# The modulation matrix summed in three column passes instead of four, and c laid out to the partitions by transfers instead of matrix products

## What is computed

```
silu_c = jax.nn.silu(c)                                    # c * sigmoid(c), 2048 values
sh1, sc1, g1, sh2, sc2, g2 = jnp.split(silu_c @ w_mod + b_mod, 6)      # w_mod: 2048 x 12288
h = modulate(rms_norm(x, norm_g[0]), sh1, sc1)
x = x + g1 * rms_norm(fourier_mix(h) @ fnet_w_out, norm_g[1])
x = x + g2 * rms_norm(sqrelu_mlp(modulate(rms_norm(x, norm_g[2]), sh2, sc2), w_mlp_in, w_mlp_out), norm_g[3])
```

## Time and profile before

| | |
|---|---|
| runs, median (lowest to highest) | 1681.84 us (1681.52 to 1683.0) |
| profiled execution, span from first to last instruction | 1678.7 us; of this execution the page gives the span alone |
| PE, DVE, ACT busy | 1667.0 us, 1190.8 us, 858.7 us |
| TensorE clock granted | 9 (full) in each of the 40 slices of the span |
| read from HBM | 404.58 MB, 242 GB/s over the span |

### The profile page before, as it was taken

The page is one execution under the profiler, slowest core; times in us unless marked ns, Lnnn a source line. Parts: engine busy times, 40 slices in busy tenths (PEclk is TensorE's granted clock), DMA queues, the critical chain, the costliest instruction groups (busy, mean ns, idle before and its releaser), DMA issues.

```text
span 1678.7 us, 22570 instructions
## 1 busy us (share of the span) xinstructions
PE 1667.0 (99%) x9084; PEld 1444.9 (86%) x9084; DVE 1190.8 (71%) x1291; ACT 858.7 (51%) x1212; POOL 21.3 (1%) x34
## 2 busy tenths in 40 slices
PE   9999999999999999999999999999999999999997
PEld 9899888888989988888898888888888888888886
DVE  7878777887868777798678577777655455546555
ACT  7667556444656655644464564434443444334442
POOL 0000000000100000000000000000000000000000
PEclk9999999999999999999999999999999999999999
DMA  9689676997777777799639478887655665566553
GB/s 333 215 274 313 218 272 226 335 356 279 247 258 253 267 238 263 240 346 370 228 125 334 151 226 282 294 286 245 196 176 200 187 190 197 210 196 188 189 200 126
DMA packets 218120, 408.16 MB, mean 243 GB/s; under 512 B 9088, under 2 KB 87200, under 8 KB 217248
## 3 DMA queue, kind: packets, MB, share of 16 engines
q1 hardware_dynamic: 217520, 404.58, 70.3%
q10 hardware_dynamic: 496, 2.14, 0.3%
HBM read 404.58 MB, written 2.11 MB: 242 GB/s over the span
## 4 chain that ended last, share of the span: by engine, by line
PE 97%; issue 1%; DVE 1%; ACT 0%; DMA 0%; POOL 0%; DVEq 0%; POOLq 0%; SPq 0%; ACTq 0%
PE banks L455 96%; PE banks L1663 1%; PE banks L1625 0%; DMA modw<-in_w_mod 0%; PE banks L1634 0%; DVE X L1104 0%; DVE X L1532 0%; PE banks L1821 0%; POOL sc L674 0%; ACT junk L712 0%; DVE modacc L1139 0%; ACT junk L723 0%; ACT swap L809 0%; ACT vtmp L1017 0%; ACT vtmp L1007 0%
## 5 line engine op out<-in xcount | busy, mean ns | idle before, releaser
L451 DVE TENSOR_TENSOR wlo<-raw,whi 128x1024 fp32r<-128x1024 f32 (+2 forms) x561 | 663.4, 1189 | 375.0 <-ACT whi L444 372.1
L444 ACT ACTIVATE whi<-raw 128x1024 fp32r<-128x1024 f32 (+2 forms) x561 | 573.4, 1030 | 578.4 <-PE banks L455 542.6
L455 PE MATMUL banks<-H,whi 128*128 128x512 f32 x2048 | 660.0, 398 | 0.7 <-DVE H L1062 0.7
L455 PEld LDWEIGHTS banks<-H,wlo 128*128 128x128 f32 x2048 | 384.9, 188 | 88.5
L455 PE MATMUL banks<-whi,Y 128*128 128x512 f32 x1472 | 455.6, 389 | 0.0
L455 PE MATMUL banks<-H,wlo 128*128 128x256 f32 x2048 | 402.6, 278 | 0.0
L455 PEld LDWEIGHTS banks<-whi,Y 128*128 128x128 f32 x1472 | 276.3, 188 | 57.7 <-DVE wlo L451 0.2
L455 PEld LDWEIGHTS banks<-H,whi 128*128 128x128 f32 x2048 | 317.0, 189 | 1.9 <-issue 0.8
L455 PE MATMUL banks<-wlo,Y 128*128 128x512 f32 x768 | 298.8, 389 | 0.0
L1139 DVE SCALAR_TENSOR_TENSOR modacc<-modw,cvx,modacc 128x1024 f32<-128x1024 f32 x188 | 240.4, 1279 | 9.7 <-DMA modw<-in_w_mod 9.4
L455 PEld LDWEIGHTS banks<-wlo,Y 128*128 128x128 f32 x768 | 144.2, 188 | 29.8
(11 more groups left out here) (224 smaller groups left out, 1343.5 us busy)
## 6 DMA issues: line engine op xcount, KB each, us to landing
modw<-in_w_mod SPq DMA_DIRECT2D x192, 512.0 KB, 6.5
raw<-in_w_in SPq DMA_DIRECT2D x72, 1024.0 KB, 5.4
raw<-in_w_mlp_in SPq DMA_DIRECT2D x64, 1024.0 KB, 5.5
raw<-in_w_mlp_out SPq DMA_DIRECT2D x64, 1024.0 KB, 5.0
raw<-in_w_o SPq DMA_DIRECT2D x32, 1024.0 KB, 7.1
raw<-in_w_fnet SPq DMA_DIRECT2D x16, 1024.0 KB, 5.1
raw<-in_w_mv SPq DMA_DIRECT2D x7, 1024.0 KB, 6.3
raw<-in_w_mk SPq DMA_DIRECT2D x6, 1024.0 KB, 6.1
```

The source lines that it names most:

```text
L444: nc.scalar.activation(hi_part(step, n), raw[u % RAW][:, (step % 2) * n:(step % 2) * n + n], ACT.Copy).then_inc(hi_ready, 1)
L451: nc.vector.tensor_tensor(wlo[u % RAW][:, part], raw[u % RAW][:, part], hi_part(step, n).bitcast(F32), ALU.subtract).then_inc(lo_ready, 1)
L455: return nc.tensor.matmul(o, a, b, start=start, stop=stop, skip_group_check=True)
```

## The change

- `MOD_PASS` has three passes: eight pieces of 1024 columns side by side for columns 0 to 8191 (128 units of 16 rows), then two passes of two pieces as before. The sums stand at steps 255 (step 111 of layer 1), 310 and 421.
- c is loaded ten times by SP, each time with the 128 partitions in the order that the units need: eight transfers for the eight-piece layout and two for the two-piece one. In each the source repeats a row for the partitions that share it. ACT and DVE make silu from all 160 columns, straight into `cvx`.
- The six products on PE, the copy on ACT and the two `alike` copies on DVE go. `sel` has 8 + 2 columns.

```diff
-MOD_PASS = ((0, 4, 0), (2 * D, 2, 64), (3 * D, 4, 96), (5 * D, 2, 160))
+MOD_PASS = ((0, 8, 0), (4 * D, 2, 128), (5 * D, 2, 160))
...
-                                sp.dma_start(cv[:, 0:KT], cvec).then_inc(c_in, 16)
+                                for c0, groups in ((0, 8), (8, 2)):
+                                    for j in range(groups):
+                                        rows_of = cvec[j * P // groups:(j + 1) * P // groups, :]
+                                        sp.dma_start(c_rows[:, (c0 + j) * KT:(c0 + j + 1) * KT],
+                                                     rows_of.unsqueeze(1).broadcast_to([P // groups, groups, KT])).then_inc(c_in, 16)
...
-                        act.wait_ge(c_in, 16)
-                        nc.scalar.activation(cv[:, KT:2 * KT], cv[:, 0:KT], ACT.Exp, scale=-1.0).then_inc(c_exp, 1)
-                    if l == 0 and s == CV_AT[3]:
-                        act.wait_ge(cv_T, 1)
-                        nc.scalar.activation(cvx[:, :], M[2][:, 0:96], ACT.Copy).then_inc(cv_ready, 1)
+                        act.wait_ge(c_in, 160)
+                        nc.scalar.activation(c_gate[:, :], c_rows[:, :], ACT.Exp, scale=-1.0).then_inc(c_exp, 1)
...
-                co = (0 if groups == 4 else 64) + j - j0
+                co = (0 if groups == 8 else 8 * KT) + (j - j0) % groups * KT + (j - j0) // groups
...
-                        for e0, groups in ((0, 4), (4, 2)):
-                            nc.vector.tensor_reduce(sel[:, e0:e0 + groups], ident[:, :].rearrange("p (i e) -> p e i", e=groups), AX_X, ALU.add)
-                            w = nc.vector.tensor_copy(alike[:, P * e0:P * (e0 + groups)].rearrange("p (i e) -> p i e", e=groups),
-                                                      ident[:, :].unsqueeze(2).broadcast_to([P, P, groups]))
+                        for e0, groups in ((0, 8), (8, 2)):
+                            w = nc.vector.tensor_reduce(sel[:, e0:e0 + groups], ident[:, :].rearrange("p (i e) -> p e i", e=groups), AX_X, ALU.add)
...
-                    if l == 0 and s == CV_AT[2]:
-
-                        pe.wait_ge(cv_step, 3)
-                        pe.wait_ge(sel_set, 1)
-                        for c0, e0, groups in ((0, 0, 4), (64, 4, 2)):
-                            for j in range(groups):
-                                i = mm(M[2][:, c0 + j:c0 + groups * KT:groups], alike[:, (e0 + j) * P:(e0 + j + 1) * P],
-                                       cv[:, 2 * KT:], True, True)
-                        i.then_inc(cv_T, 1)
```

More of the change, by code:

```diff
@@ L211 @@
 MOD_END = {c: step for step, c in MOD_SUM.items()}
-CV_AT = (4, 5, 9, 10)
+CV_AT = (4, 5)
 ANG_AT = (6, 8, 12, 15)
 GATE_ROW = (114, 116, 118, 121)
-assert MOD_END[1] < LH + GATE_ROW[0] and MOD_END[2] < BY_TOKEN[1]
+assert MOD_END[0] < LH + GATE_ROW[0] and MOD_END[1] < BY_TOKEN[1]
 IDLE = 24
@@ L324, in build_program @@
         ones = at("ones", [P, 8], m + 0.5)
-        sel = at("sel", [P, 8], m + 0.53125)
         gs = at("gs", [P, G_CONST], m + 0.5625)
-        alike = at("alike", [P, 6 * P], A + 50)
+        c_rows = at("c_rows", [P, 10 * KT], A + 50)
+        c_gate = at("c_gate", [P, 10 * KT], A + 51)
         modT = at("modT", [P, NMOD * KT], m + 0.8125)
@@ L335, in build_program @@
         A2 = at("A2", [P, KT], m + 1.6875)
-        cv = at("cv", [P, 3 * KT], m + 1.75)
-        ropev = at("ropev", [P, 2], m + 1.9375)
-        sc = at("sc", [P, 96], m + 1.96875)
+        sel = at("sel", [P, 10], m + 1.75)
+        ropev = at("ropev", [P, 2], m + 1.8125)
+        sc = at("sc", [P, 96], m + 1.84375)
         SS, MS, RS = 0, 4, 8
@@ L345, in build_program @@
         PS, PN, XP, XN = 64, 5, 80, 3
-        cvx = at("cvx", [P, 96], m + 2.34375)
-        assert origin + (m + 2.71875) * 1024 <= nc.sbuf_top
+        cvx = at("cvx", [P, 10 * KT], m + 2.21875)
+        assert origin + (m + 2.84375) * 1024 <= nc.sbuf_top
         banks = ctx.enter_context(nc.psum_tensor("banks", [P, 8, 512], F32))
@@ L355, in build_program @@
         pair = [flat_banks[:, 1024 * i:1024 * (i + 1)] for i in range(4)]
-        MODCOL = 480
+        MODCOL = 448
         def bank(g):
@@ L395, in build_program @@
         x_copied, x_sum, conv_in, conv_out = map(sem, ("x_copied", "x_sum", "conv_in", "conv_out"))
-        sel_set, cv_T, cv_ready = sem("sel_set"), sem("cv_T"), sem("cv_ready")
+        sel_set = sem("sel_set")
         x2_T0, x2_T1, x2_hi0, x2_lo0 = map(sem, ("x2_T0", "x2_T1", "x2_hi0", "x2_lo0"))
@@ L1128, in mod_unit @@
                 dve.wait_ge(mod_in[j % MRING], 16 * (j // MRING + 1))
-                co = (0 if groups == 4 else 64) + j - j0
+                co = (0 if groups == 8 else 8 * KT) + (j - j0) % groups * KT + (j - j0) // groups
                 co = cvx[:, co:co + 1]
                 if j == 0:
-                    dve.wait_ge(cv_ready, 1)
+                    dve.wait_ge(cv_step, 3)
                 if j == j0:
@@ L1284, in _ @@
                         dve.wait_ge(c_exp, 1)
-                        nc.vector.tensor_scalar(cv[:, KT:2 * KT], cv[:, KT:2 * KT], 1.0, None, ALU.add).then_inc(cv_step, 1)
+                        nc.vector.tensor_scalar(c_gate[:, :], c_gate[:, :], 1.0, None, ALU.add).then_inc(cv_step, 1)
                         dve.wait_ge(cv_step, 1)
-                        nc.vector.reciprocal(cv[:, 2 * KT:], cv[:, KT:2 * KT]).then_inc(cv_step, 1)
+                        nc.vector.reciprocal(cvx[:, :], c_gate[:, :]).then_inc(cv_step, 1)
                         dve.wait_ge(cv_step, 2)
-                        tt(cv[:, 2 * KT:], cv[:, 2 * KT:], cv[:, 0:KT], ALU.mult).then_inc(cv_step, 1)
+                        tt(cvx[:, :], cvx[:, :], c_rows[:, :], ALU.mult).then_inc(cv_step, 1)
                         dve.wait_ge(ident_in, 16)
-                        for e0, groups in ((0, 4), (4, 2)):
-                            nc.vector.tensor_reduce(sel[:, e0:e0 + groups], ident[:, :].rearrange("p (i e) -> p e i", e=groups), AX_X, ALU.add)
-                            w = nc.vector.tensor_copy(alike[:, P * e0:P * (e0 + groups)].rearrange("p (i e) -> p i e", e=groups),
-                                                      ident[:, :].unsqueeze(2).broadcast_to([P, P, groups]))
+                        for e0, groups in ((0, 8), (8, 2)):
+                            w = nc.vector.tensor_reduce(sel[:, e0:e0 + groups], ident[:, :].rearrange("p (i e) -> p e i", e=groups), AX_X, ALU.add)
                         w.then_inc(sel_set, 1)
@@ L1392, in _ @@
                     if l == DEPTH - 1 and s == GATE_ROW[0]:
-                        dve.wait_ge(mod_out, 2)
+                        dve.wait_ge(mod_out, 1)
                         tt(R[:, 0:KT], mod(2), ng(1), ALU.mult).then_inc(r_ready, 1)
@@ L1440, in _ @@
                     scaled_rows(acc[i % 2], rowb, i, 2 * (4 * DEPTH + i)).then_inc(acc_dve, 1)
-            dve.wait_ge(mod_out, 3)
+            dve.wait_ge(mod_out, 2)
             nc.vector.scalar_tensor_tensor(A2[:, :], mod(4), 1.0, ng(2), ALU.add, ALU.mult)
@@ L1489, in _ @@
                     if q == 2 and s == 2:
-                        dve.wait_ge(mod_out, 4)
+                        dve.wait_ge(mod_out, 3)
                         tt(R[:, KT:], mod(5), ng(3), ALU.mult).then_inc(r_ready, 1)
@@ L1586, in mod_sums @@
                 pe.wait_ge(sel_set, 1)
-                own = sel[:, 0:4] if groups == 4 else sel[:, 4:6]
+                own = sel[:, 0:8] if groups == 8 else sel[:, 8:10]
                 for t in range(8):
@@ L1618, in _ @@
                             pe.wait_ge(x_xn, 2 * l + 2)
-                            pe.wait_ge(cv_ready, 1)
                             sums_read(base + s)
@@ L1825, in _ @@
             by_token(1, acc[1], (Hhi, Hlo))
-            pe.wait_ge(mod_out, 3)
+            pe.wait_ge(mod_out, 2)
             pe.wait_ge(acc_dve, DVE0 + 3)
```

## The result

The changed kernel takes **1751.76 us** (median of five runs, 1748.23 to 1761.24), the kernel before 1681.8 (1681.5 to 1683.0). The ratio is 1.0425, interval 1.0409 to 1.044: slower by 70 us where 1.9 us less was forecast. The profiled execution is the longest of the five, 1761.24 with a span of 1759.4 us.

What follows compares the result with a forecast made beforehand. The prediction took TensorE (PE), busy 99% of the span, to bound the kernel. Products -1.34, sum pass -1.80 and delay +1.2 summed to -1.9 us, giving 1679.9 us, range 1678.2 to 1682.8.

Steps and rivals of the forecast that it cites:

- At nothing: Items priced at zero: copies removed on ACT and DVE, three longer DVE operations, the reshaped w_mod loads, moved steps.
- the four rivals: Alternative outcomes: 1678.7 us (chance 0.20), 1681.3 (0.10), 1696.6 (0.06) and 1681.7 (0.09).
- The chance of slower, 0.08: Probability given to a time over 1685.20 us, slower by more than 0.2%.
- SP's issue: Rival at c's ten transfers: slow issues on SP's queue delay step 8's unit by 17.9 us, 1696.6 us; chance 0.06.
- a fixed cost of the small transfers: Rival: each of nine extra transfers costs the DMA engines 0.29 us, delay 2.6, kernel 1681.3 us; chance 0.10.
- The sum pass, -1.80: PE in attention, step 63 of layer 1: one of four passes of eight sum products goes, -1.80 us.
- rival 4: In attention, step 63 of layer 1, softmax sets the pace and the sum's 1.80 us return: 1681.7 us; chance 0.09.
- The products, -1.34: PE at about 31.5 us: the six products that lay c out go, -1.34 us.
- The delay d, +1.2: Step 8 of layer 0: c's ten transfers make the w_mk unit land later, PE stands still, +1.2 us (ends 0 and 1.8).
- the page's figure, 1684.8: Kernel time in us if nine more small transfers cost 6.1 us, estimated by the skill page; not the forecast.
- a gap above 3 us at step 8: Sign of being wrong: PE's gap at step 8, 0.15 us before and forecast about 1.3, exceeds 3 us.
- new waits of PE after step 14: Sign of being wrong: PE shows waits after step 14 that the kernel before did not have.

Runs made afterwards that it cites:

- the control of the last: Kernel before with one unit of w_mod moved from step 50 to step 63 in layer 0 alone: 1681.05 us, ratio 0.9993.
- the fourth: Kernel before without the products, four passes, c's transfers behind unit 7's load, one w_mod unit moved from step 50 to 63 in both layers: 1683.47 us.
- its control: Kernel before with one unit of w_mod moved from step 50 to step 63 in both layers, nothing else: 1684.14 us, ratio 1.0013.
- the first experiment: Changed kernel with the four passes of before, c still laid out by transfers, six in place of ten: 1681.31 us, ratio 0.9998.
- the changed kernel with fast loads: Changed kernel with first-pass loads of 32 half rows of four pieces, from other columns of w_mod, in place of 16 rows of eight: 1683.5 us.

## Why the prediction was wrong

**The step that failed** stands under *At nothing*: "The 192 loads of w_mod keep their size of 512 KB; a load has 16 rows of eight pieces in place of 32 of four, and the pieces stay 4 KB." It was priced at zero because bytes, packets and pieces stay. The trace of before had loads of 32 rows of four and 64 of two, and none of 16 rows, so this was an operation that it didn't show, and it was given no bounds. By itself the form costs 0.8 us for each of 128 loads; the kernel pays 68 us in all for it, in PE's waits and in products at half clock behind them. None of the four rivals had it. The chance of slower, 0.08, was put on SP's issue and on a fixed cost of the small transfers, neither of which makes the 70 us.

**The sum pass, -1.80**, holds. PE's timeline at step 63 of layer 1, the place of rival 4, before and then with three passes, half rows and c late:

```profile
581.72 0.60 PE L1663 MATMUL banks<-ident,prob 128*128 128x128 f32 x4
582.15 1.84 PE L455 MATMUL banks<-sel,modacc 128*128 128x2 f32 x16
583.86 0.48 PE L455 MATMUL banks<-H,whi 128*128 128x512 f32 x1
```

```profile
582.77 0.60 PE L1657 MATMUL banks<-ident,prob 128*128 128x128 f32 x4
583.12 0.48 PE L455 MATMUL banks<-H,whi 128*128 128x512 f32 x1
```

From the transposes of prob to the next product 2.14 us become 0.35, 1.79 less, where 1.80 was read from the earlier trace rows. By SP's issues of weights this kernel keeps that lead until step 111 of layer 1. There it pays 1.81 for the sum of eight columns, against 1.84 that went with the sum of four at step 128, so eight columns cost no more. Rival 4, that the time comes back in attention, falls by this trace. In the time of whole runs the sum doesn't stand out: three passes against four give -0.9 against +0.1 us with c late, and -2.7 against -1.3 with the unit moved (in layer 0 alone for the second); that is 1.0 and 1.4 us less, with intervals of 1.5 us either way on each of the four.

**The products, -1.34**, are right as what PE is held at 31 us and wrong as what the run gains: in the traces PE is 1.5 us early at 34 us and not at all at 152, behind the wait for kn. Of the four kernels with four passes and no products, three differ from the kernel before by -0.6, +0.1 and -1.3 us, and the control of the last, with the products, by -1.2; the fourth, with the sum at 208, is 2.0 slower and its control 2.7. In time what is left of the 1.34 can't be told from nothing. That PE waited for nothing there did not mean that what stands behind it had 1.3 us to spare.

**The delay d, +1.2**, had the right mechanism and was too small. SP's timeline of the changed kernel from c to the unit of step 8, with its issue for step 16; PE's weight load of step 8; and the window around it, with the clock:

```profile
14.60 6.43 SPq L610 DMA_DIRECT2D c_rows<-in_cvec  x10
...
23.83 0.43 SPq L410 DMA_DIRECT2D raw<-in_w_mk  x1
...
39.38 0.37 SPq L410 DMA_DIRECT2D raw<-in_w_in  x1
```

```profile
31.89 0.28 PEld L455 LDWEIGHTS banks<-memh,whi 128*128 128x128 f32 x1 [3.34 <-issue]
```

```profile
28.00:36.00 8.00, 5.06 (x27) 4.59 (x26) 5.63 (x13) 5.89 (x8) 0.00 (x0) 0.79 1.03 406
```

An issue took 6.43 / 10 = 0.64 us where 0.48 to 0.61 was read from the earlier trace rows, the unit was issued at 23.83 and not at 21.6 to 22.8, and landed 5.5 us later where 5.0 was assumed. PE's gap is 3.34 in place of 0.15, 3.2 us; the clock of 0.79 over the 8 us around it costs some 8 x 0.21 = 1.7 more. The issue for step 16 is 3.45 late, and with the products' 1.34 that makes 4.8, four times d. It does not grow evenly: with six transfers in the first experiment the unit was issued at 20.12 and the gap was 0.45 us. In time the ten cost 2.4 us against their late place (above). The Trainium skill, page "DMA: Bandwidth & Descriptors", section "Rules for kernel authors", advises against many small transfers. For nine more the prediction estimated 6.1 us from that page, which is too much where its own 1.2 was too little. That the sum with the page's figure, 1684.8, is nearer to the 1683.5 of the changed kernel with fast loads than the forecast of 1679.9 is in part luck: both sums count the products' 1.34, which the runs don't show.

Two signs named in advance were seen and pointed the right way: a gap above 3 us at step 8, and new waits of PE after step 14.

## What to carry to other kernels

A load is priced by its form as well as its bytes: how many outer rows it has and which partitions they fall on. If a change gives a load a form that the trace doesn't show, that is an unknown price times the number of loads, and a few such transfers alone settle it. Where DVE waits only ten microseconds for 192 loads and PE for none, transfers may be just fast enough, and a rate nearly 40% lower comes through. And where a planner sets places by counting, moving one unit may move something else: read the places again.

## What the runs showed of the hardware

Loads of 512 KB in pieces of 4 KB to 128 partitions ran at 385 to 407 GB/s with 32 to 128 outer rows, at 240 with 16, at 128 with eight. With 16 the DMA engines count as fully occupied (1.03), with eight as half (0.51). 64 partitions from 0 on took 210 GB/s, 64 from 32 on 347. Two halves of a load from two queues were faster than from one, 315 against 241 GB/s. After 4.4 us without work TensorE came back at a granted clock of 0.50 and was at 1.00 about 4 us later.
